# A long one-core transformer kernel on Trainium2: eight matmuls on zeros removed from the head of TensorE's program

## What is computed

```python
h = jnp.concatenate([meta, x], axis=1)                 # 272 x 1024
y = xf * lax.rsqrt(jnp.mean(xf * xf, axis=-1, keepdims=True) + RMS_EPS) * gain
x_rnn, gate, q, k, v = jnp.split(y @ w_in, SPLIT_AB, axis=-1)
```

## Time and profile before

| what | value |
|---|---|
| runs of the kernel | 2090.59, 2091.63, 2095.22 us; median 2091.63 |
| profiled execution | 2093.58 us, its span 2091.8 us |
| outside the span in that execution | 1.78 us |
| mean granted TensorE clock | 0.991 |
| TensorE busy in matmuls | 2032.9 us, 97% of the span |
| VectorE, ScalarE, GpSimd busy | 1180.2, 995.2 and 276.5 us |
| read from HBM | 340.61 MB, 163 GB/s over the span |

### The profile page before, as it was taken

How to read it: one execution, slowest core, us unless ns; L and a number is a source line. 1 busy time by engine, 2 the same in 40 slices (tenths; PEclk the granted TensorE clock), 3 DMA queues, 4 the chain that set the end, 5 groups by cost and what they waited for, 6 DMA issues and landing times.

```text
span 2091.8 us, 27859 instructions
## 1 busy us (share of the span) xinstructions
PE 2032.9 (97%) x11862; PEld 1772.5 (85%) x11862; DVE 1180.2 (56%) x1106; ACT 995.2 (48%) x1074; POOL 276.5 (13%) x194
## 2 busy tenths in 40 slices
PE   8999999999999999999999999999999999999998
PEld 7789999998999988877877778887887887777887
DVE  6754446756654455545556865546555555776553
ACT  5743434344544354445355564435444535556443
POOL 4114401413344110002100010001000210001000
PEclk8999999999999999999999999999999999999999
DMA  7245545532555555545533445555554553345552
GB/s 199 78 131 172 180 170 195 177 125 101 177 182 184 181 181 185 193 167 180 181 121 121 161 161 181 185 177 179 183 181 161 189 173 121 121 161 167 192 181 104
DMA packets 195154, 343.17 MB, mean 164 GB/s; under 512 B 14074, under 2 KB 97308, under 8 KB 194924
## 3 DMA queue, kind: packets, MB, share of 16 engines
q1 hardware_dynamic: 194404, 339.73, 49.0%
q0 software_dynamic: 368, 0.79, 0.2%
q10 hardware_dynamic: 280, 1.16, 0.2%
HBM read 340.61 MB, written 1.05 MB: 163 GB/s over the span
## 4 chain that ended last, share of the span: by engine, by line
PE 81%; DVE 8%; ACT 7%; DMA 3%; issue 1%; POOL 0%; SPq 0%; DVEq 0%; POOLq 0%; ACTq 0%
PE banks L474 15%; PE banks L477 15%; PE banks L475 15%; PE banks L318 6%; PE banks L319 6%; PE banks L320 6%; PE banks L369 5%; DVE w_lo L311 2%; PE banks L1588 2%; PE banks L1589 2%; PE banks L1590 2%; ACT w_hi L304 2%; DMA raw<-w_in 1%; ACT e L2292 1%; PE banks L513 1%
## 5 line engine op out<-in xcount | busy, mean ns | idle before, releaser
L311 DVE TENSOR_TENSOR w_lo<-raw,w_hi 128x2048 fp32r<-128x2048 f32 x320 | 754.4, 2359 | 596.4 <-ACT w_hi L304 595.8
L304 ACT ACTIVATE w_hi<-raw 128x2048 fp32r<-128x2048 f32 x320 | 611.4, 1913 | 675.3 <-DMA raw<-ffn_wd 152.3
L474 PE MATMUL banks<-w_hi,xn_hi 128*128 128x512 f32 x1248 | 493.7, 396 | 11.3 <-DVE w_lo L311 10.6
L475 PE MATMUL banks<-w_lo,xn_hi 128*128 128x512 f32 x1248 | 487.1, 390 | 0.0
L477 PE MATMUL banks<-w_hi,xn_lo 128*128 128x512 f32 x1248 | 482.2, 391 | 0.0
L474 PEld LDWEIGHTS banks<-w_hi,xn_hi 128*128 128x128 f32 x1248 | 234.9, 188 | 63.9 <-DVE w_lo L311 14.8
L477 PEld LDWEIGHTS banks<-w_hi,xn_lo 128*128 128x128 f32 x1248 | 234.8, 188 | 49.7
L475 PEld LDWEIGHTS banks<-w_lo,xn_hi 128*128 128x128 f32 x1248 | 235.0, 188 | 45.9
L318 PE MATMUL banks<-xn_hi,w_hi 128*128 128x272 f32 (+1 forms) x720 | 208.8, 290 | 4.9 <-DVE xn_lo L425 4.9
L320 PE MATMUL banks<-xn_hi,w_lo 128*128 128x272 f32 (+1 forms) x720 | 207.0, 287 | 0.0
L319 PE MATMUL banks<-xn_lo,w_hi 128*128 128x272 f32 (+1 forms) x720 | 206.5, 287 | 0.0
(11 more groups left out here) (343 smaller groups left out, 2962.8 us busy)
## 6 DMA issues: line engine op xcount, KB each, us to landing
raw<-w_in SPq DMA_DIRECT2D x60, 1024.0 KB, 5.1
raw<-ffn_w_gu SPq DMA_DIRECT2D x44, 1024.0 KB, 5.1
raw<-ffn_wd SPq DMA_DIRECT2D x44, 1024.0 KB, 4.8
raw<-ffn_wg SPq DMA_DIRECT2D x40, 1024.0 KB, 5.1
raw<-ffn_wu SPq DMA_DIRECT2D x40, 1024.0 KB, 5.1
raw<-ret_w_in SPq DMA_DIRECT2D x24, 1024.0 KB, 5.3
raw<-ffn_w_down SPq DMA_DIRECT2D x22, 1024.0 KB, 4.9
raw<-ret_w_out SPq DMA_DIRECT2D x8, 1024.0 KB, 4.9
```

What stands on the lines that cost most here:

```text
L304: nc.scalar.activation(w_hi[:, n0 % SLOTS, :], raw[:, n0 % SLOTS, :], ACT.Copy).then_inc(S["w_hi"], 1)
L311: nc.vector.tensor_tensor(w_lo[:, n0 % SLOTS, :], raw[:, n0 % SLOTS, :], w_hi[:, n0 % SLOTS, :].bitcast(F32), ALU.subtract).then_inc(S["w_ ...
L474: pe.matmul(ps[:, (b + n) * 512:(b + n + 1) * 512], xh, h, start=start, stop=False)
L475: pe.matmul(ps[:, (b + n) * 512:(b + n + 1) * 512], xh, o, start=False, stop=False)
```

## The change

The wait for `memd` and the eight matmuls behind it are taken out of `pe_start()`. TensorE's first instruction that waits is now the wait for `in_x`. Nothing else differs: `hsq` is still cleared at the same place of VectorE's program, and `memd` still counts.

```diff
         def pe_start():
 
-            pe.wait_ge(S["memd"], 1)
-            for _ in range(8):
-                pe.matmul(ps[:, 7 * 512:7 * 512 + 256], hsq[:, 0, 0:P], hsq[:, 0, 0:256], start=True, stop=True)
             pe.wait_ge(S["in_x"], 64)
             for kt in range(KT):
                 b = kt * 512
```

## The result

The changed kernel took 2096.97 us (median of 11 runs, 2094.38 to 2099.78), the kernel before 2093.18 us beside it (11 runs, 2090.49 to 2095.22). The ratio is 1.0020, with a 95% interval of 1.0012 to 1.0028: slower by 3.8 us. The forecast was no change, 2091.6 us in a range of 2088.4 to 2095.2 us.

A forecast was written before the change was run, and what follows sets the result against it. TensorE, busy 97% of the span, was taken as the bound, with the input's DMA setting the pace up to 9.5 us. All terms summed to 0 on 2093.58 us; moved to the runs' median: 2091.6 us, range 2088.4 to 2095.2.

The forecast's parts named there:

- Points 1 and 2: Kernel head: removing the `memd` wait and eight matmuls (6.00 us of TensorE) is hidden behind the input's DMA, worth 0.
- Point 3: Clock at the transposes: they ran at the lower level anyway, so loss 0 to 0.41 us, taken as 0.
- the clock sometimes lasted: Raised clock held through transposes or to the first products in some earlier executions; price 2.14 us, giving 2093.8 us; chance 0.07.
- Point 4: Clock at the first products from 19.30 us: already lower despite the zeros, so loss 0 to 1.73 us, taken as 0.
- Point 5: Contention of the zeros' reads with the input's DMA: removal gains 0 to 2.29 us, taken as 0.
- the later dips move: Later stretches at 1.2 GHz under busy TensorE change length, 3.2 us either way, 2088.4 to 2094.8 us; chance 0.03.

The follow-up runs named there:

- before again: The kernel before, unchanged, measured once more against itself: 2093.03 us, ratio 1.0000.
- the two cut kernels with eight: The kernel before, its eight matmuls on zeros kept, cut off behind the first mixer (137.63 us) or behind the retention layer (570.00 us).
- the full and the cut kernel with twelve: Twelve matmuls on zeros in place of eight, in the kernel before (2093.65 us, ratio 0.9999) and in it cut behind the first mixer (138.08 us).
- the cut kernels: Kernel before and changed kernel, later stages left out: behind the first mixer 137.63 and 139.02 us, behind the retention layer 570.00 and 572.44 us (again 571.83).
- tiny zeros: The kernel before with its eight matmuls on zeros at 16 columns instead of 256: ratio 1.0008, again 1.0004; cut short, 139.28 and 571.83 us.
- waits only: The changed kernel with 33 waits for `memd` put before TensorE's wait for `in_x`: 2095.66 us, ratio 1.0004 to the kernel before.

## Why the prediction was wrong, point by point

- **Points 1 and 2 held.** The wait and the matmuls were not on the path, and their removal started nothing earlier. What the sum had no term for is that 32 fewer instruction records on TensorE (27859 and 27827 in all) move the later transfers of instructions against the work.
- **Point 3 failed, and with it the price of the rival "the clock sometimes lasted".** I took 0 because the profiled execution had lost the raised clock at 9.55 us, and set a bound of 0.41 us from the landing of the weights in that one execution. Both were properties of one execution. In the five other profiles with full zeros and real transposes the level lasted into the transposes or through them: they took 5.23 us (before again) and 4.31 us (the two cut kernels with eight, the full and the cut kernel with twelve) in place of 6.74 us. The weights landed anywhere from before 13.54 to 16.49 us. The term is up to 2.4 us on TensorE. In the cut kernels the first product came earlier by 0.8 us (17.79 and 18.59 us) and 1.8 us (17.23 and 19.00 us), but not by the transposes alone: the second pair's weights were split from 13.87 and from 15.64 us, both after waiting for the DMA, and these 1.77 us are the landing. The landings overlap between kernels with and without the zeros, so I take them for luck.
- **Point 4 failed too: it was 0 where it should have been a gain lost.** The earlier start went on into an earlier return of the clock: 19.9 to 23.2 us in the profiles with full zeros and real transposes, 22.8 to 25.2 us in those without any, with tiny ones and with waits only. Points 3 and 4 together measure 1.4 us by the medians at 138 us and 2.0 us by record 600 of the profiles. My bounds of 0.41 and 1.73 us held the sum; the chance of 0.07 that I gave the case did not. Five of six profiles were of this kind, and the one I had was the exception.
- **Point 5 held at 0.** The transposes started at 8.87 us against 9.54 us in the first profiles, but with zeros also at 8.71 and 8.97 us, without at up to 9.20 us and with tiny ones at 9.38 us.
- **The rival "the later dips move" was taken for luck, and that failed.** I priced a dip at 3.2 us either way and gave 0.03 to a systematic shift. The full kernels lose 2.9 to 3.8 us by the medians, and the start accounts for 1.4 to 2.0 us. In the stretch from 1833 to 1909 us all three profiles of the changed kernel lose 3.6 us or more, some 1.3 us by a late chunk of weights and the rest by dips; at 504 us they gain 1.5 to 4.6 us. With tiny zeros the late stretch costs 1.5 to 1.8 us and with waits only nothing, which fits their medians between the two kernels. That the way through the first 25 us shifts all later work against the moments at which the clock may change would explain the dips, and it is argued, not shown; a dip behind a longer pause of TensorE would as well. How often each dip comes over many executions stays open.
- **The range and the threshold.** The range leaned on three runs and one profile. Its upper end was the highest of the three; the kernel before itself reached 2098.14 us in later samples. I took 0.2% for what a measurement can tell from no change. With eleven runs each the interval was 0.08% to either side, so that the 3 us of a few small terms could be told.

The page of the Trainium skill cited ahead (TensorE: Matmul & The Clock Gate, "What's actually happening") says that the moments of change shift from run to run. The profiles agree: 6.1 and 5.3 us for the first rise and 9.6 and 12.2 us for the fall in two executions of the same kernel. I had cited it and priced it within one execution's bounds; it should have turned the weighing round.

## What to carry to other kernels

Work that does nothing but raise the clock can't be judged from one profile: look at the level in several executions, and weigh the one at hand as a draw. A bound that rests on when a transfer landed is a bound for that execution only. To place an effect at the head of a long kernel, cut the kernel behind it; to place the rest, look up the same record in the profiles of the full kernels and see in which stretch the times between starts part. An edit at the head also moves everything that goes by the count of instructions. A variant with the instructions but not their work (here the tiny zeros and the waits) is what tells the two apart.

## What the runs showed of the hardware that was not expected

- Transposes run faster at the raised clock (4.31 us for 24, against 6.73 us) but did not raise it themselves in 6.73 us. Nor did 48 records of float32 products by the identity in 13.56 us.
- Transfers of a kernel's own instructions share the profile with its data: with one of 16 KB in the midst of it, a 1 MB chunk of weights took 6.4 us in three profiles, and without 5.0 to 5.4 us in nine. That the one caused the other is inferred.
- Until the first recorded change a profile lists the clock as 1.00, whatever it is: 17 records in 3.80 us stood under 1.00. The mean clock of the changed kernel reads higher (0.993 against 0.991) though it lost more time to the clock.
- Segments without a dip repeated closely: the 2750 records from 650 to 3400 took 351.5 to 351.9 us in nine profiles. What differs between executions of a kernel of 2.1 ms lies in its start and in the stretches with dips, four to seven of 3.4 to 10.2 us in each full profile.
